# First conditioning weights loaded into idle buffers, and the first pair's query and key products formed depth by depth during the loads

## The reference, cut to what matters

```python
    cond = jax.nn.silu(c)
    cond_ctx = jax.nn.silu(c_ctx)
    for l in range(DEPTH):
        shift, scale, gate = jnp.split(cond @ w_ada[l] + b_ada[l], 3, axis=-1)
        shift_c, scale_c, gate_c = jnp.split(cond_ctx @ w_ada[l] + b_ada[l], 3, axis=-1)
        h = x * (1.0 + scale[:, None]) + shift[:, None]
        hc = cx * (1.0 + scale_c) + shift_c
        ...
```

```python
    q = heads(qa, GLA_HEADS) * (GLA_DK ** -0.5)
    z = jnp.einsum('btdr,drk->btdk', lr, gla_gate_w) + gla_gate_b
    g = jax.nn.log_sigmoid(z.astype(F32)) / GLA_TAU
```

## Time and profile before

| | us |
|---|---|
| three runs, median | 1793.4 |
| lowest, highest | 1789.64, 1794.16 |
| the profiled execution | 1788.54 |
| its span | 1786.5 |
| TensorE busy | 1643.3 (92%) |
| VectorE, ScalarE busy | 640.9, 566.2 |
| mean granted TensorE clock (1 is 2.4 GHz) | 0.971 |

### The profile page before, as it was taken

The page is one execution under the profiler, slowest core; times in us unless marked ns, Lnnn a source line. Parts: engine busy times, 40 slices in busy tenths (PEclk is TensorE's granted clock), DMA queues, the critical chain, the costliest instruction groups (busy, mean ns, idle before and its releaser), DMA issues.

```text
span 1786.5 us, 25259 instructions
## 1 busy us (share of the span) xinstructions
PE 1643.3 (92%) x9836; PEld 985.8 (55%) x9836; DVE 640.9 (36%) x1401; ACT 566.2 (32%) x1277; POOL 82.1 (5%) x143
## 2 busy tenths in 40 slices
PE   4999999889999999889999888999999899999995
PEld 2476766555656565554554347586655355555442
DVE  2113424421513214331114563134344355554144
ACT  0222222332413324432112342213134365554024
POOL 0000000000000000000011100000000011111111
PEclk7999999989999999999999899999999999999997
DMA  8100021110313023000224310001000000001322
GB/s 344 68 25 24 13 84 60 53 66 31 124 59 131 12 72 119 24 13 27 74 93 154 106 70 36 12 13 37 24 25 24 13 19 7 25 13 39 109 82 100
DMA packets 33348, 108.32 MB, mean 61 GB/s; under 512 B 3536, under 2 KB 5840, under 8 KB 31952
## 3 DMA queue, kind: packets, MB, share of 16 engines
q1 hardware_dynamic: 27792, 97.27, 14.8%
q10 hardware_dynamic: 5440, 9.44, 1.4%
HBM read 97.26 MB, written 9.44 MB: 60 GB/s over the span
## 4 chain that ended last, share of the span: by engine, by line
PE 71%; issue 16%; DVE 6%; ACT 4%; DMA 1%; POOL 1%; ACTq 0%; SPq 0%; POOLq 0%; DVEq 0%
PE proj L888 27%; PE mixed L888 13%; PE proj L871 4%; PE mixed L871 4%; PE mixed L990 3%; PE turned L976 3%; PE scores L1084 2%; PE scores L956 2%; ACT work L1522 2%; PE scores L1110 1%; DMA weights<-in_weights 1%; PE scores L959 1%; PE turned L1121 1%; ACT yT L1522 1%; DVE kvV L1483 1%
## 5 line engine op out<-in xcount | busy, mean ns | idle before, releaser
L888 PE MATMUL proj<-hT,weights 128*128 128x512 f32 (+1 forms) x1376 | 553.9, 549 | 11.5 <-ACT kvV L1522 2.6
L888 PEld LDWEIGHTS proj<-hT,weights 128*128 128x128 f32 x1376 | 256.2, 194 | 236.8 <-issue 226.7
L888 PE MATMUL mixed<-hT,weights 128*128 128x512 f32 (+1 forms) x416 | 175.2, 565 | 1.7 <-ACT kvV L1522 1.7
L888 PE MATMUL proj<-yT,weights 128*128 128x512 f32 x320 | 141.1, 592 | 0.0
L1522 ACT ACTIVATE work<-work,stat 128x640 f32<-128x640 f32 (+8 forms) x144 | 108.8, 755 | 41.7 <-DVE stat L1285 37.9
L888 PEld LDWEIGHTS mixed<-hT,weights 128*128 128x128 f32 x416 | 77.4, 192 | 77.2 <-issue 74.4
L888 PE MATMUL mixed<-yT,weights 128*128 128x512 f32 (+1 forms) x320 | 115.0, 512 | 0.0
L1522 ACT ACTIVATE work<-turned 128x512 f32<-128x512 f32 (+2 forms) x136 | 72.8, 535 | 109.1 <-PE turned L972 98.4
L976 PE MATMUL turned<-consts,work 128*128 128x128 f32 (+4 forms) x656 | 99.8, 279 | 7.9 <-ACT work L1522 7.9
L976 PEld LDWEIGHTS turned<-consts,work 128*128 128x128 f32 (+4 forms) x656 | 74.8, 139 | 54.4 <-issue 33.6
L1379 DVE SCALAR_TENSOR_TENSOR work<-work,turned 128x128 f32<-128x128 f32 (+1 forms) x152 | 53.1, 349 | 142.3 <-PE turned L1121 139.1
(11 more groups left out here) (223 smaller groups left out, 1966.4 us busy)
## 6 DMA issues: line engine op xcount, KB each, us to landing
weights<-in_weights SPq DMA_DIRECT2D x131, 512.0 KB, 3.3
tables<-in_bias SPq DMA_DIRECT2D x8, 1281.0 KB, 7.8
hT<-in_xT SPq DMA_DIRECT2D x8, 640.0 KB, 9.3
work<-in_xT SPq DMA_DIRECT2D x16, 256.0 KB, 3.3
x1T<-yT ACTq DMA_DIRECT2D x8, 512.0 KB, 2.7
work<-x1T SPq DMA_DIRECT2D x16, 256.0 KB, 3.3
out<-yT ACTq DMA_DIRECT2D x8, 512.0 KB, 2.8
tables<-in_tables SPq DMA_DIRECT2D x1, 1792.0 KB, 7.3
```

The source lines that it names most:

```text
L888: last = nc.tensor.matmul(PJ[BANK_OF[u]][:, 0:n], weights[:, w % WBUFS, k, :], src[:, k, t0:t0 + n], start=(k == 0), stop=(k == KT - 1))
```

## The change

The sixteen conditioning tiles of the first four groups leave the ring of five buffers. They go to buffers of their own in `yT`, `work` and slot 1 of `pair`, all idle at that time, and SyncE issues them without a wait, group by group, each followed by the two input tiles that it serves; behind the first group come the query and key weights of pair 0, which now stand at the head of `PLAN`. The small loads (`lr_w`, `gate_w`, the constants) and the next three weight tiles come behind all of that.

The queries and keys of pair 0 are no longer formed piece by piece. A new step `early` takes one input tile as soon as it is modulated and adds its depth to all six pieces, which fill the banks `SC[0]`, `MI`, `OV` and both `TP` together. Depth 0 stands behind the first group, depths 1 and 2 behind the second, 3 and 4 behind the third, 5 to 7 behind the fourth. ScalarE copies the six pieces out in a new step `early_copy`. The conditioning products and turns of these groups share the second bank of `SC`. The low-rank product stands whole behind `early_copy`, and the ten gate products stand between the five pieces of values alone. The first of them waits for the query and key copies.

```diff
@@ make_schedule
-    s, early = [("setup",)], project(("lr",), "lr", CHUNKS_ALL)
+    s, depth = [("setup",)], 0
     for x in range(0, KT, 2):
         s += [("ada", 0, ada_first(x), None), ("ada_turn", 0, ada_first(x), None), ("modulate", x), ("modulate", x + 1)]
-        if x:
-            s += [early[x // 2 - 1], early[4 + x // 2 - 1]]
-    s += [early[3], early[7]]
-    s += early[8:] + between(qkv("gla", 0), [("gate0", t) for t in range(NT)])
+        while depth < (x + 1 if x + 2 < KT else KT):
+            s.append(("early", depth))
+            depth += 1
+    s += [("early_copy",)] + project(("lr",), "lr", CHUNKS_ALL)
+    s += between(values("gla", 0), [("gate0", t) for t in range(NT)])
...
-PLAN = []
+FIRST = [("ada", 0, _f) for _s in SCHEDULE if _s[0] == "ada" and _s[3] is None for _f in _s[2]]
+PLAN = [("gla", 0, "q"), ("gla", 0, "k")]
...
+        first_at = ([yT[:, :, :].rearrange("p k t -> p (k t)")[:, x * D:(x + 1) * D] for x in range(8)]
+                    + [work[:, x * D:(x + 1) * D] for x in range(4)]
+                    + [pair[:, 1, x * D:(x + 1) * D] for x in range(4)])
...
+        def early_bank(w, t0):
+            if t0 == 0:
+                return SC[:, 0:CTX] if w == "q" else SC[:, CTX:2 * CTX]
+            return ((MI, OV) if w == "q" else TP)[chunk_no(t0) - 1][:, :]
@@ sync
+            for g in range(4):
+                for n in range(4 * g, 4 * g + 4):
+                    sp.dma_start(first_weights(n), a["weights"][len(PLAN) + n]).then_inc(
+                        *up(f"first_loaded{g}", *([("first", g)] if n % 4 == 3 else []), by=16))
+                load_x(2 * g)
+                load_x(2 * g + 1)
+                if g == 0:
+                    load_weights(2)
+            sp.dma_start(vstage[:, 0, 0:256], a["lr_w"]).then_inc(*up("lr_loaded", ("lr_loaded",), by=16))
...
             load_weights(WBUFS)
-            load_x(0)
-            load_x(1)
-            sp.dma_start(vstage[:, 0, 0:256], a["lr_w"]).then_inc(*up("lr_loaded", ("lr_loaded",), by=16))
             for s in SCHEDULE:
-                if s[0] == "ada":
+                if s[0] == "ada" and s[3] is not None:
                     load_weights(WEIGHT_AT[("ada", s[1], s[2][0])] + WBUFS)
-                    if s[3] is None:
-                        load_x(s[2][1] + 1)
-                        load_x(s[2][1] + 2)
...
@@ tensor
+            def s_early(k):
+
+                pe.wait_ge(*at(("modulated", k)))
+                for n, w in enumerate(("q", "k")):
+                    if k == 0:
+                        pe.wait_ge(*at(("weight", n)))
+                    for t0, m in CHUNKS_ALL:
+                        last = nc.tensor.matmul(early_bank(w, t0), weights[:, n, k, :], hT[:, k, t0:t0 + m],
+                                                start=(k == 0 and (w == "q" or t0 > 0)), stop=(k == KT - 1),
+                                                skip_group_check=True)
+                    if k == KT - 1:
+                        done(last, ("early", w), ("weight_used", n))
...
@@ tensor, gate0
                     pe.wait_ge(*at(("loaded", "consts")))
+                    for w in ("q", "k"):
+                        pe.wait_ge(*at(("filled", "gla", 0, w)))
@@ scalar
+            def s_early_copy():
+                def copy(w, t0, n, keys=()):
+                    run((pq if w == "q" else pk)(0)[:, t0:t0 + n], early_bank(w, t0), ACT.Copy, keys,
+                        scale=QSCALE if w == "q" else 1.0)
+
+                act.wait_ge(*at(("early", "q")))
+                for t0, n in CHUNKS_LAT:
+                    copy("q", t0, n)
+                act.wait_ge(*at(("early", "k")))
+                copy("q", 0, CTX, [("filled", "gla", 0, "q")])
+                for t0, n in CHUNKS_ALL:
+                    copy("k", t0, n, [("filled", "gla", 0, "k")] if t0 + n == T else [])
```

More of the change, by code:

```diff
@@ L411 @@
 SCHEDULE = make_schedule()
-PLAN = []
+FIRST = [("ada", 0, _f) for _s in SCHEDULE if _s[0] == "ada" and _s[3] is None for _f in _s[2]]
+PLAN = [("gla", 0, "q"), ("gla", 0, "k")]
 for _s in SCHEDULE:
     for _k in [("ada", _s[1], _f) for _f in _s[2]] if _s[0] == "ada" else [_s[1]] if _s[0] == "mm" else []:
-        if _k != ("lr",) and _k not in PLAN:
+        if _k not in FIRST and _k != ("lr",) and _k not in PLAN:
             PLAN += [_k, (*_k[:2], "v1")] if _k[2:] == ("v0",) else [_k]
@@ L767, in load_x @@
                     sp.dma_start(hT[:, k, :], a["xT"][k]).then_inc(*up(f"x_loaded{k}", ("x", k), by=16))
+            for g in range(4):
[7 more added lines that the diff above has]
+            sp.dma_start(vstage[:, 0, 0:256], a["lr_w"]).then_inc(*up("lr_loaded", ("lr_loaded",), by=16))
+            for name, dst, src in (("gate_w", gate_w[:, :], a["gate_w"]),
+                                   ("consts", consts[:, P:CONST_W], a["consts"][:, P:CONST_W])):
+                sp.dma_start(dst, src).then_inc(*up("constants_loaded", ("loaded", name), by=16))
             load_weights(WBUFS)
-            load_x(0)
-            load_x(1)
-            sp.dma_start(vstage[:, 0, 0:256], a["lr_w"]).then_inc(*up("lr_loaded", ("lr_loaded",), by=16))
             for s in SCHEDULE:
-                if s[0] == "ada":
+                if s[0] == "ada" and s[3] is not None:
                     load_weights(WEIGHT_AT[("ada", s[1], s[2][0])] + WBUFS)
-                    if s[3] is None:
-                        load_x(s[2][1] + 1)
-                        load_x(s[2][1] + 2)
[L779 to L782, removed]
                 if s[0] == "mm" and s[7] == 0:
@@ L821, in s_ada @@
             def s_ada(l, fs, u):
[L823 to L826, removed]
+                if u is None:
+                    tiles_of = [first_weights(FIRST.index(("ada", l, f))) for f in fs]
+                    pe.wait_ge(*at(("first", fs[0] // 2)))
+                    if ada_before(l, fs):
+                        pe.wait_ge(*at(("mods", *ada_before(l, fs))))
+                    used = []
+                else:
+                    ns = [WEIGHT_AT[("ada", l, f)] for f in fs]
+                    tiles_of = [weights[:, n % WBUFS, :, :] for n in ns]
+                    for n in ns:
+                        pe.wait_ge(*at(("weight", n)))
                     wait_bank(pe, u)
+                    used = [("weight_used", n) for n in ns]
                 for k in range(KT):
-                    for g, n in enumerate(ns):
+                    for g, tile in enumerate(tiles_of):
                         last = nc.tensor.matmul(ada_bank(fs, u)[32 * g:32 * (g + 1), :], cond_wide[:, k, :],
-                                                weights[:, n % WBUFS, k, :], start=(k == 0), stop=(k == KT - 1))
-                done(last, ("ada", l, fs[0]), *[("weight_used", n) for n in ns])
+                                                tile[:, k, :], start=(k == 0), stop=(k == KT - 1))
+                done(last, ("ada", l, fs[0]), *used)
+            def s_early(k):
+                pe.wait_ge(*at(("modulated", k)))
+                for n, w in enumerate(("q", "k")):
+                    if k == 0:
+                        pe.wait_ge(*at(("weight", n)))
+                    for t0, m in CHUNKS_ALL:
[4 more added lines that the diff above has]
+                        done(last, ("early", w), ("weight_used", n))
             def s_ada_turn(l, fs, u):
@@ L881, in s_mm @@
                     if dest == "lr":
-                        if t0 <= CTX:
-                            pe.wait_ge(*at(("modulated", k)))
+                        pe.wait_ge(*at(("modulated", k)))
                         rows = slice(32 * (k % 3), 32 * (k % 3 + 1))
@@ L1867, in weight_tiles @@
     lr = columns(("lr",))[:, 0:32].reshape(KT, P, 32).transpose(1, 0, 2).reshape(P, KT * 32)
-    return np.stack([columns(k).reshape(KT, P, P).transpose(1, 0, 2) for k in PLAN]), np.ascontiguousarray(lr)
+    return np.stack([columns(k).reshape(KT, P, P).transpose(1, 0, 2) for k in PLAN + FIRST]), np.ascontiguousarray(lr)
 def bias_tables(rpb):
```

16 lines of the change are left out of this document (7 added, 9 removed).

## The result

The changed kernel takes 1770.4 us in the median of four runs (1768.24 to 1773.31), against 1793.6 for the kernel before, run beside it. The ratio is 0.9878, with a 95% interval of 0.986 to 0.9895. The forecast was 1778.8 in a range from 1772.0 to 1784.4: the direction was right, the gain was larger than forecast and the time lies under the range. The profiled executions, 1788.54 and 1768.24 us, are 20.3 us apart, and their spans 20.4; that is what the traces can explain, and the forecast for it was 14.6. The interval puts the gain in the medians at 18.8 to 25.1 us, so the two agree.

The account below looks back on a forecast made before the run. Loads were taken to bound the first 50 us, TensorE what follows. A gain of 16.9 us less 1.15 (gates) and 1.2 (clock) gave 14.6, so 1793.4 - 14.6 = 1778.8 us, range 1772 to 1784.4.

Parts of the forecast that it names:

- SyncE's queue: At the loads: 30 transfers take 16 us to issue, each moving data for 1.3 to 1.6 us, so issuing keeps ahead.
- values begin before, without gates: Kernel before, at the values: start at 93.20 us less 5.16 for six gate products, giving 88.04.
- depth 0 beyond 4.30, lost to the clock: At the start: TensorE idle from 14.5 to 16.4 us may lower its clock, costing 0 to 2.4, taken as 1.2 us.
- loss ahead of the scan: Before the scan: with gates in pairs, ScalarE has two to do at the end, losing 1.15 us.
- A conditioning group does not care: Conditioning groups take the same time at either clock: 3.68 us for the first, 3.64 at 0.50.
- part (b): TensorE's clock at the start: an added cost between nothing and 2.4 us, taken as 1.2 us.
- A gain isn't possible: TensorE's clock at the start: it can bring no gain, since 88.04 was reached at 1.00.
- The slack at group two: Group two's loads are there at 19.2 us and TensorE comes at 20.7, leaving 1.5 us.
- the margin for the banks: Depth products: each going to another bank than the one before costs nothing; 0.7 us over all depths allowed in the range.
- Late loads: Rival at the first group: it finishes only with the four transfers issued behind it, everything 4.4 us later, 1783.2; chance 0.09.
- The low clock: Rival at the depths: all eight run at 1.2 GHz, costing another 34.4 us, 1812.0; chance 0.05.
- No change: Rival behind the moved products: the gain is lost again, time within 5.4 us of 1793; chance 0.06.

Follow-up runs that it names:

- the added tiles: The changed kernel with two more tiles (1.05 MB, read by nobody) loaded ahead of group two's; ran once, in 1770.9 us.
- the extra products: The changed kernel plus products whose result nobody reads, eight ahead of the first group and four behind its turn; 1770.8 us, ratio 0.9876.
- spreading the gates: The changed kernel with one gate product behind each of the first ten quarters of the values instead of pairs behind the pieces; 1769.3 us, ratio 0.9883.
- the second comparison: The changed kernel unchanged, run once more on one chip beside two other versions and the kernel before; 1773.8 us, ratio 0.9899.
- extra products and hold: The changed kernel plus unread products around group one, with SyncE issuing nothing behind group two's tiles until they landed; 1772.1 us, ratio 0.9897.
- with the gates one by one: The changed kernel with extra products and hold, and single gate products behind quarters of the values; 1767.8 us, ratio 0.987; again, 1766.8 us, ratio 0.986.

## Why the prediction was right in direction and wrong in size

Right were the bound (loads until 50 us, TensorE behind it), the depth at 4.30 us, the low-rank product at 6.5 (60.57 to 67.14), the loads no longer binding behind group one, and the rest of the program moving forward whole. SyncE's queue bound nothing either, but not as worked out: the issues slowed down, four conditioning tiles taking 5.24 and then 6.46 us, and the 29 transfers took until 29.8 us instead of 16, while the DMA engines stayed full. The terms of the sum, against the profile after:

| term, as the prediction put it | forecast us | measured us |
|---|---|---|
| values begin before, without gates | 88.04 | 88.90 |
| depth 0 starts | 16.4 | 15.99 |
| depth 0 beyond 4.30, lost to the clock | 1.2 | 2.0 |
| groups two to four, with copy and turn | 3 x 4.58 | 3 x 2.75 |
| loss ahead of the scan | 1.15 | 1.37 |
| gain at the scan | 14.6 | 20.4 |

**The step that failed is "A conditioning group does not care: 3.68 us for the first, 3.64 for the one at 0.50."** It cost 5.5 of the 5.8 us by which the gain at the scan was missed, 5.1 on three groups and the rest mostly on their turns (0.30 us each instead of 0.39). I took the 1.00 in the clock column for the clock of the first group. But the first clock entry in the trace of the kernel before stands at 13.71 us, after that group, and ahead of the first entry the column prints 1.00. A group takes 1.93 us at the higher clock. Three runs show it: in the changed kernel the first group drops from 3.64 to 1.95 when products run ahead of it, the four groups of the kernel before drop to 1.95 to 2.62, and with the changed kernel's loads and buffers but waits ahead of the groups they stay at 2.7 to 3.6. So part (b) had the wrong sign, and "A gain isn't possible" with it: against prices at the lower clock I counted a cost of 1.2 us, and the clock brought 3.5, 5.5 on the groups less 2.0 on depth 0.

That is the Trainium skill's rule (TensorE: Matmul & The Clock Gate, "Loop structure matters more than you think") seen from its other side. The page says that a long DMA wait between matmuls leaves the engine cold and that back-to-back products keep it warm; the kernel before was its bad case, and the change, though it goes one K-tile (one depth) at a time, filled the waits. The trace agrees with the rule's reason and not with its loop order: the granted clock is 1.00 from 22 to 100 us, over depths 1 to 7.

**A slip of 0.86 us**: five gate products stand ahead of the values, as the earlier trace rows and my own sentence before it had it, and I took off six.

**The slack at group two** was given as 1.5 us, from two numbers that were both off: TensorE comes at 22.18 instead of 20.7, and in the executions where group two waited for the tiles it started at 21.28 to 21.65, not at 19.2. That leaves 0.5 to 0.9 us (the added tiles alone would give up to 1.7). The errors largely cancelled, which is luck, and the step did no harm here; but it misjudges a kernel that comes earlier, as the extra products showed.

**Ahead of the scan** the mechanism and the size were right (3.36 us of wait against 3.3), and spreading the gates showed it. The 1.37 in the table also holds a first piece of values that took 7.10 us instead of 6.91.

**The range** ends 1.6 us above the measured time, and that it comes so close is luck: its lower end takes off, besides the full gain of 15.8 us, the 4.9 us by which one execution lay under the median. The gain itself was to be 15.8 us at most, 16.5 with the margin for the banks, and was 20.4.

**The rivals.** Late loads: the first group, for which the rival was worked out, began at 9.66 us, 0.4 before the forecast and not 4.4 behind it. Group two's tiles were indeed 2 us later than the order of issue gives, but not for the reason named, and it cost nothing. The low clock: depth 0 lost 2.0 us to it in part of its run, far from the 3.7 depths from which it would decide. No change: excluded by the interval.

What stays between the traces' 20.4 us and the medians' 23.1 is scatter between executions; the second comparison gave 18.5.

## What to carry to other kernels

When TensorE waits in short pieces, price not only the waits but also the work between them at the higher clock: filling a wait can nearly halve what stands behind it. Take an instruction's duration at each clock from two places whose clock is known from another instruction beside them, such as a wide product, and not from the clock column near the program's start. And a transfer lands with its slowest engine, so compare landings with landings rather than with bytes over the total rate.

## What the runs showed of the hardware

- The granted clock shown is 1.00 from the span's start until the trace's first clock entry, whatever the engine does: that entry stands at 13.71 us in the kernel before, at 13.76 in the changed kernel and at 22.14 in its repeat. In the repeat wide products took twice their time with 1.00 beside them from 16.5 to 21 us. In the same kernel the first group took 3.64 us at 1.00, and with products ahead of it 1.95 at 1.00.
- 32 conditioning products of 128 columns, 32 columns wide in the stationary operand, take 1.93 us at the higher clock and 3.64 at the lower; between them stand 2.60 to 3.54, where it changed on the way.
- After a wait of 2.8 us with the same work ahead of it, the granted clock fell to 0.50 in one execution and stayed at 1.00 in another (extra products and hold, without and with the gates one by one).
- Of sixteen DMA engines one was behind the others where all later loads were held back, in two of three executions; in the third, two were until 20.4 us. With extra products and hold, when 6.7 MB had been asked for and nothing followed, the DMA share fell to 0.66 in 18 to 20 us and to 0.06, one engine, in 20 to 21, and the transfer had landed only at 21.5.
- SyncE's issues slowed with many transfers outstanding: four tiles took 1.85 us to issue at 1.63 us, 5.24 at 8.71 and 6.46 at 16.23, in the changed kernel.
